# A linear-recurrence stage on one core: the first product of each level by 128x128 block matrices, and an identity added by VectorE

## What is computed

```python
def rwkv7_recurrence(r, decay, k, v, kk, a):       # 8 heads, 256 steps, 64x64 state
    def step(state, inp):
        r_t, w_t, k_t, v_t, kk_t, a_t = inp
        sa = jnp.einsum('bhij,bhj->bhi', state, -kk_t)
        state = (state * w_t[:, :, None, :]
                 + sa[..., :, None] * (kk_t * a_t)[..., None, :]
                 + v_t[..., :, None] * k_t[..., None, :])
        return state, jnp.einsum('bhij,bhj->bhi', state, r_t)
```

## Time and profile before

| what | us |
|---|---|
| median of 3 runs (2218.88 to 2220.39) | 2220.13 |
| span of the profiled execution | 2214.8 |
| around the span (median less span) | 5.3 |
| PE busy in the span | 2114.3 (95%) |
| DVE busy | 1195.3 (54%) |
| ACT busy | 766.2 (35%) |

### The profile page before, as it was taken

One profiled execution on the slowest core, in us unless ns is written; L12 is line 12 of the kernel. 1 busy time (PEld: TensorE's weight loads), 2 busy tenths in 40 slices (PEclk: granted clock), 3 DMA queues, 4 the chain that ended last, 5 costly groups with the idle time before them and its releaser, 6 DMA issues. The chain is left out here.

```text
span 2214.8 us, 34331 instructions
## 1 busy us (share of the span) xinstructions
PE 2114.3 (95%) x14251; PEld 1462.8 (66%) x14251; DVE 1195.3 (54%) x1882; ACT 766.2 (35%) x1011; POOL 16.9 (1%) x18
## 2 busy tenths in 40 slices
PE   7988999999998999999999999999999999999999
PEld 5767744333334433334437888988888888988888
DVE  5774513322222222223327876888765874888874
ACT  3553301111011100011105554556544553656543
POOL 0000000000000000000000000000000000000000
PEclk9999999999999999999999999999999999999999
DMA  9544699999999999999996555444655655444652
GB/s 373 185 165 198 258 416 430 428 431 430 431 429 430 429 430 430 428 430 431 430 427 215 191 194 167 155 147 147 199 191 186 194 190 190 152 136 133 209 191 76
DMA packets 200264, 625.87 MB, mean 283 GB/s; under 512 B 13200, under 2 KB 150352, under 8 KB 164304
## 3 DMA queue, kind: packets, MB, share of 16 engines
q1 hardware_dynamic: 197536, 622.41, 72.4%
q10 hardware_dynamic: 2608, 1.72, 0.3%
HBM read 623.05 MB, written 1.05 MB: 282 GB/s over the span
## 5 line engine op out<-in xcount | busy, mean ns | idle before, releaser
L2259 DVE TENSOR_TENSOR w_low<-ring,w_high 128x2048 fp32r<-128x2048 f32 x168 | 386.6, 2306 | 164.3 <-ACT w_high L2254 164.3
L2254 ACT ACTIVATE w_high<-ring 128x2048 fp32r<-128x2048 f32 x168 | 320.3, 1910 | 172.7 <-PE bank L2608 139.8
L2603 PE MATMUL bank<-h_both,w_high 128*128 128x512 f32 x1344 | 322.5, 392 | 0.0
L1965 PE MATMUL bank<-ring,ut 128*64 128x512 f32 x1024 | 249.3, 640 | 35.4 <-DMA ring<-in_exp_w_dram 35.4
L2603 PEld LDWEIGHTS bank<-h_both,w_high 128*128 128x128 f32 x1344 | 246.6, 188 | 48.9
L2054 ACT ACTIVATE sg<-glu 128x512 f32<-128x512 f32 x32 | 20.2, 630 | 567.6 <-DVE glu L2127 567.6
L1932 PE MATMUL bank<-ring_odd,xt 128*64 128x512 f32 x960 | 209.7, 594 | 2.9 <-DVE lin L2130 2.3
L1932 PE MATMUL bank<-ring,xt 128*64 128x512 f32 x960 | 209.3, 594 | 0.0
L1965 PEld LDWEIGHTS bank<-ring,ut 128*64 128x64 f32 x1024 | 74.2, 147 | 194.6 <-issue 132.3
L2143 DVE SCALAR_TENSOR_TENSOR xT<-bank,mod,xT 128x256 f32<-128x256 f32 x128 | 54.2, 477 | 224.4 <-PE bank L1976 224.4
L2608 PEld LDWEIGHTS bank<-h_both,w_low 128*128 128x128 f32 x1344 | 167.4, 188 | 7.0
(11 more groups left out here) (571 smaller groups left out, 2779.8 us busy)
## 6 DMA issues: line engine op xcount, KB each, us to landing
ring<-in_exp_w_dram SPq DMA_DIRECT2D x64, 2048.0 KB, 27.7
ring_odd<-in_exp_w_dram SPq DMA_DIRECT2D x64, 2048.0 KB, 27.8
ring<-in_exp_w_dram SPq DMA_DIRECT2D x128, 1024.0 KB, 25.4
ring<-in_ffn_w_gate_dram SPq DMA_DIRECT2D x44, 1024.0 KB, 5.2
ring<-in_ffn_w_up_dram SPq DMA_DIRECT2D x44, 1024.0 KB, 5.2
ring<-in_ffn_w_down_dram SPq DMA_DIRECT2D x44, 1024.0 KB, 4.9
ring<-in_w_in_dram SPq DMA_DIRECT2D x36, 1024.0 KB, 5.2
ring<-in_ada_w_dram SPq DMA_DIRECT2D x24, 1024.0 KB, 9.8
```

What stands on the lines that cost most here:

```text
L1965: ins = nc.tensor.matmul(bank[first + dh][at:at + 64, :], ut[:, r % 4, rows:rows + 64], w[:, x, 512 * dh:512 * dh + 512], start=False, sto ...
L2254: nc.scalar.activation(w_bufs[0][u % BUFS], ring2[:, u % RING2, :], ACT.Copy).then_inc(high2, 1)
L2259: nc.vector.tensor_tensor(w_bufs[1][u % BUFS], ring2[:, u % RING2, :], w_bufs[0][u % BUFS].bitcast(F32), ALU.subtract).then_inc(low2, 1)
L2603: return nc.tensor.matmul(b[:, :], w_parts[0][:, at:at + P], moving.rearrange("p a t -> p (a t)"), start=start, stop=False, skip_group_che ...
```

## The change

1. `low` becomes `low_blocks`: for each system a 128x128 matrix with the two 64x64 triangles in two quarters and zeros in the other two. It lies in the memory of `states`. GpSimd clears the zero quarters with four memsets at the stage's start; ACT writes the triangles with four copies of 64 partitions in place of two of 128.
2. `x_product` is then one product over all 128 rows in place of two over 64.
3. The groups are systems 0 to 7 and 8 to 15 (contiguous) in place of even and odd.
4. The 32 identity products are gone. DVE adds the identity while it takes the step matrices from PSUM (four instructions); ACT's eight copies are gone.
5. DVE's work on `bonus` and `gate` moves behind the first and the second `state`; ACT's clears of `states` in level 4 move behind the levels.

```diff
-                def x_product(s_, ph):
-                    return nc.tensor.matmul(place(4 + s_ % 2, inverse_rows(s_, ph), s_), low[half_rows(ph), s_, :], inv_t[half_rows(ph), s_, :],
-                                            start=True, stop=True)
+                def x_product(s_):
+                    return nc.tensor.matmul(place(4 + s_ // (NS // 2), slice(0, P), s_), low_blocks[:, s_, :], inv_t[:, s_, :], start=True, stop=True)
...
-                        pe.wait_ge(sem("low_ready"), 2)
+                        pe.wait_ge(sem("low_cleared"), 4)
+                        pe.wait_ge(sem("low_ready"), 2 * g + 2)
...
-                    for s_ in range(0, NS, 2):
+                    for s_ in range(NS // 2):
                         for ph in range(2):
                             grown = growth_t(s_, ph)
-                        for ph in range(2):
-                            ins = x_product(s_ + 1, ph)
+                        ins = x_product(NS // 2 + s_)
...
-                        for h2 in range(2):
-                            for ph in range(2):
-                                r = half_rows(ph)
-                                ins = nc.tensor.matmul(bank[6 + ph][half_rows(h2), at:at + 64], ident[r, r], ident[r, r], start=False, stop=True)
...
-                        for a in range(TT):
-                            ins = nc.scalar.activation(step_m[rows, 2 * a + ph, :, rows],
-                                                       bank[6 + ph][rows, T * a:T * a + T].rearrange("p (h j) -> p h j", h=HP), ACT.Copy)
-                        st.tell(ins, "m_taken")
...
+                dve.wait_ge(sem("cleared"), 1)
+                dve.wait_ge(sem("m_ready"), 1)
+                for ph in range(2):
+                    for h2 in range(2):
+                        rows = half_rows(h2)
+                        st.tell(nc.vector.tensor_tensor(step_m[rows, ph:NCH:2, :, rows], bank[6 + ph][rows, :].rearrange("p (a h j) -> p a h j", a=TT, h=HP),
+                                                        ident[rows, rows].unsqueeze(1).unsqueeze(1).to_broadcast([64, TT, HP, 64]), ALU.add), "m_taken")
```

More of the change, by code:

```diff
@@ L1079, in build @@
             a3, a2, a4 = lt_a3[:, :, 1, :], a2_a4[:, :, 0, :], a2_a4[:, :, 1, :]
-            low, inv, inv_t, xs = (x.rearrange("p (s t) -> p s t", t=CH) for x in ring_scratch[4:8])
+            inv, inv_t, xs = (x.rearrange("p (s t) -> p s t", t=CH) for x in ring_scratch[5:8])
             za = ring[:, SCRATCH + 2, :].rearrange("p (s x) -> p s x", s=NS)
@@ L1087, in build @@
             states = sb("states", [P, NCH, HP, P], where=c5)
+            low_blocks = states[:, :, :, :].rearrange("p c h t -> p (c h) t")
             LEVELS = 5
@@ L1105, in inverse_rows @@
             def inverse_rows(s_, ph):
-                return half_rows(ph if s_ % 2 else 1 - ph)
+                return half_rows(ph if s_ >= NS // 2 else 1 - ph)
             def group(x, g):
-                return x[:, g:NS:2, :]
+                return x[:, NS // 2 * g:NS // 2 * g + NS // 2, :]
             def chunks(ap, ph):
@@ L1114, in build, with _ @@
             SYSTEMS = [(h2, hp, a) for h2 in range(2) for hp in range(HP) for a in range(TT)]
+            @S.block.gpsimd
+            def _(gps):
+                S.clear_former(gps)
+                for g in range(2):
+                    for ph in range(2):
+                        nc.gpsimd.memset(group(low_blocks, g)[half_rows(ph), :, half_rows(ph if g == 0 else 1 - ph)], 0.0).then_inc(S.sem("low_cleared"), 1)
             @S.block.sync
@@ L1137, in place @@
                 def place(b, rows, s_):
-                    return bank[b][rows, CH * (s_ // 2):CH * (s_ // 2) + CH]
-                def x_product(s_, ph):
-                    return nc.tensor.matmul(place(4 + s_ % 2, inverse_rows(s_, ph), s_), low[half_rows(ph), s_, :], inv_t[half_rows(ph), s_, :],
-                                            start=True, stop=True)
+                    return bank[b][rows, CH * (s_ % (NS // 2)):CH * (s_ % (NS // 2)) + CH]
+                def x_product(s_):
+                    return nc.tensor.matmul(place(4 + s_ // (NS // 2), slice(0, P), s_), low_blocks[:, s_, :], inv_t[:, s_, :], start=True, stop=True)
                 def growth_t(s_, ph):
                     r = inverse_rows(s_, ph)
-                    return nc.tensor.matmul(place(2 + s_ % 2, half_rows(ph), s_), inv[r, s_, :], xs[r, s_, :], start=True, stop=True)
+                    return nc.tensor.matmul(place(2 + s_ // (NS // 2), half_rows(ph), s_), inv[r, s_, :], xs[r, s_, :], start=True, stop=True)
                 def wait_x(n, g):
@@ L1166, in growth @@
                         pe.wait_ge(sem("products_taken"), 2)
-                    for s_ in range(g, NS, 2):
+                    for s_ in range(NS // 2 * g, NS // 2 * g + NS // 2):
                         for ph in range(2):
@@ L1197, in _ @@
                 wait_x(0, 0)
-                for s_ in range(0, NS, 2):
-                    for ph in range(2):
-                        ins = x_product(s_, ph)
+                for s_ in range(NS // 2):
+                    ins = x_product(s_)
                 ins.then_inc(sem("x_ready0"), 1)
@@ L1221, in _ @@
                         wait_x(n + 1, 0)
-                    for s_ in range(0, NS, 2):
+                    for s_ in range(NS // 2):
                         for ph in range(2):
-                            grown = growth_t(s_ + 1, ph)
+                            grown = growth_t(NS // 2 + s_, ph)
                         if n + 1 < LEVELS:
-                            for ph in range(2):
-                                ins = x_product(s_, ph)
+                            ins = x_product(s_)
                     grown.then_inc(sem("growth_t1"), 1)
@@ L1261, in _ @@
                                 r = half_rows(ph)
-                                nc.tensor.matmul(bank[6 + ph][half_rows(h2), at:at + 64], za[r, system(h2, hp, a), 0:64],
-                                                 nat[r, 1, a, head_cols(h2, hp)], start=True, stop=False)
-                        for h2 in range(2):
-                            for ph in range(2):
-                                r = half_rows(ph)
-                                ins = nc.tensor.matmul(bank[6 + ph][half_rows(h2), at:at + 64], ident[r, r], ident[r, r], start=False, stop=True)
+                                ins = nc.tensor.matmul(bank[6 + ph][half_rows(h2), at:at + 64], za[r, system(h2, hp, a), 0:64],
+                                                 nat[r, 1, a, head_cols(h2, hp)], start=True, stop=True)
                 ins.then_inc(sem("m_ready"), 1)
@@ L1344, in _ @@
                 act.wait_ge(sem("low_product"), 1)
-                for h2 in range(2):
-                    st.tell(nc.scalar.activation(flat(low[:, 8 * h2:8 * h2 + 8, :]), bank[4 + h2][:, :], ACT.Copy), "low_ready")
+                for g in range(2):
+                    for ph in range(2):
+                        st.tell(nc.scalar.activation(group(low_blocks, g)[half_rows(ph), :, half_rows(1 - ph if g == 0 else ph)],
+                                                     bank[4 + g][half_rows(ph), :].rearrange("p (s t) -> p s t", t=CH), ACT.Copy), "low_ready")
                 for n in range(LEVELS):
@@ L1355, in _ @@
                     st.tell(nc.scalar.activation(a2v[:, q, :, :, :], bank[6 + q][:, :].rearrange("p (h a i) -> p h a i", h=HP, a=TT), ACT.Copy), "a2v_taken")
-                for k in range(2 * (LEVELS - 1), 12):
+                for k in range(6, 12):
                     clear(k)
@@ L1437, in _, with gate_bonus, weigh_gate @@
                     st.tell(nc.vector.tensor_copy(flat(za[:, 4 * k:4 * k + 4, :]), bank[k][:, :]), "za_taken")
[L1438 to L1443, removed]
+                def gate_bonus():
+                    for m in range(HP):
+                        ins = nc.vector.scalar_tensor_tensor(bonus[:, m, :], bonus[:, m, :], par("rwkv_gn_b", m), gate[:, m, :], ALU.add, ALU.mult)
+                    st.tell(ins, "bonus_gated")
+                def weigh_gate():
+                    dve.wait_ge(sem("bonus_gated"), 1)
+                    for m in range(HP):
+                        nc.vector.tensor_scalar(gate[:, m, :], gate[:, m, :], par("rwkv_gn_g", m), None, ALU.mult)
                 dve.wait_ge(sem("out_squares"), 1)
@@ L1453, in _ @@
                                                     chunk_decay[:, :, c:c + 1].to_broadcast([P, HP, 64]), ALU.mult), "state_ready")
+                    if c == 0:
+                        gate_bonus()
+                    elif c == 1:
+                        weigh_gate()
                 dve.wait_ge(sem("out_root"), 1)
```

5 lines of the change are left out of this document (1 added, 4 removed).

## The result

The changed kernel takes 2272.51 us (median, 2268.68 to 2280.15), the kernel before 2219.51 us in the same series: a ratio of 1.0244, 95% interval 1.0225 to 1.0262. The forecast was 2249 with a range of 2238 to 2258. The direction was right, the size was not: 53 us slower where 29 were worked out. The profiled execution has a span of 2271.0 us, 56.2 more than before's 2214.8.

What follows compares the result with a forecast made beforehand. PE waiting for its own instructions, 256 in some 3.6 us, was taken to bound the levels. Terms 29.4 + 0.5 - 0.9 = +29.0 us gave a span of 2243.8, median 5.3 above: 2249.1 us, range 2238 to 2258.

Steps and rivals of the forecast that it cites:

- Bound by refills of instructions: Levels before the change: PE waits for its own instructions, 256 of them in some 3.6 us; this bound falls away after.
- A system 0.62 us, a change of shape 0.14 us: Block of x_product and growth_t: 0.117 + 0.224 + two shape changes of 0.14; a block of eight 4.97 instead of 0.93 us.
- Rival 1: Levels: refills stay the bound and fewer instructions pay, -6.3 us, 2213.8 us, or 2217 with part of the gain; 6%.
- rival 2: Blocks of the levels: shapes change without a drain when no wait stands between; +9.4 in all, 2229.5 us; 7%.
- The levels +29.4 us: First block to values(1): 27.0 us before, 56.4 after, from slower blocks plus 0.5 for mask and copy waits.
- Rival 3: PE's clock falls in the levels as products are sparser: 2300 us at worst, +1.7 for one piece; 4% for over 2258.
- First product +0.5: Product standing alone ahead of the levels: 16 full records take 1.8 us where 16 quarter products took 1.2; +0.5 us.
- Identity by VectorE: Behind the levels: 32 identity products gone from PE, eight times 0.117 us, -0.93 us.
- 0 for the refills: Two instruction pauses behind the levels: first may become two of some 1.6 us, second is covered; 0, ends -2.9 to +3.2.
- DVE, ACT, GpSimd and the moved work at nothing: DVE's additions, ACT's copies, GpSimd's memsets, bonus and gate lie off the path: 0; additions 2.7 us if uncovered.

Runs made afterwards that it cites:

- one-column run: Kernel before with one more product of one moving column, same weights, ahead of each growth product (128 products); 2228.5 us, ratio 1.0044.

## Why the prediction failed where it did

- **Bound by refills of instructions**: it fits the traces, and the pauses did end as forecast (no "issue" idle in the levels after). The one-column run can't confirm that instructions rather than products set the 3.6 us; the sum does not need it, as it put nothing down for fewer instructions in the levels.
- **A system 0.62 us, a change of shape 0.14 us**: right. 0.63 at full clock; 0.141 and 0.146 for a change from three kernels. Rival 1 needed a half level of 2.25 us and rival 2 a block of 2.73; at full clock the changed kernel took 5.83 and 4.96.
- **The levels +29.4 us**: the term that failed; the direction was right, the size was half of what was measured. It was worked out throughout at the granted clock of 1.00, from rows at 1.00. At that clock the sum holds (56.0 us for 56.4); with 71.7 us at 0.50 the levels took 57.8 us more in place of 29.4.
- **Rival 3, the clock, at 4%**: the step behind it was wrong. It read the earlier trace rows as a clock that falls after an idle time, noted that "No idle of that length would arise", and left the sparser products as a half sentence. The clock did fall, the second time with no idle since 156.08, and stayed down for 64.86 us. Its end of 2300 us was a fair bound, but 4% and a range up to 2258 were not. What could have raised the chance: before's levels had 64 records in 1.14 us, and the change spends 45% of each system's time (0.28 of 0.62) on changes of shape. The rows read from before had no such stretch at any clock, so its 1.00 said nothing of this order.
- **First product +0.5**: right. ACT's first copy of X starts 5.86 us after the stage's first ACT work (149.37 to 155.23), before 5.38 by the same measure.
- **Identity by VectorE**: -0.93 for the products as forecast (L1263's 64 records alone, 1.16 us). "0 for the refills" was mis-sized: the second pause went, as said, but the first became one longer pause and not two of 1.6. -2.1 in all by the traces of two kernels, -3.9 (1.8 to 5.8) by the medians of one.
- **DVE, ACT, GpSimd and the moved work at nothing**: right. DVE's additions end at 250.90, PE's first reader starts at 255.67; `bonus` lies before DVE's wait of 3.23 us.

The Trainium skill, TensorE: Matmul & The Clock Gate, Part 1, ties the half clock to how busy PE has been. The rows here go half way with it: the clock did change with the work that PE was given, but PE's records filled 64.86 of 64.86 us while the clock was 0.50, so "busy" as the profile counts it did not tell whether the clock would stay.

## What to carry to other kernels

Fewer and larger products were no gain by themselves in this fp32 kernel: one full product of 64 columns cost 0.224 us where the two quarter products that it replaced cost 0.058 beside others, and each change between the two forms cost 0.14 us more. If forms must mix, try putting all of one form together: the same work in two changes for a block instead of 16 took 2226 us in place of 2272, still more than the 2218 of before. When a change makes PE's work sparser, do the sum at half clock too: half-level times differed by 1.67 between the two levels, and a PE row that is busy all the time is no sign that the clock will hold.

## What the runs showed of the hardware

- The granted clock fell to 0.50 and stayed there for 64.86 us while PE's records left no gap. It stayed at 1.00 with two changes of shape in a block of 3.0 us, was down for 10 us with eight, for 13.5 with sixteen and full products twice, for 71.7 with sixteen and single ones; and for most of the levels with two changes and 16 products of one column (0.58 on average from 182 to 277 us). The kernels with eight changes and with the full products twice fell only once, in the first block, and ran the same order at 1.00 afterwards; why they stayed up is open.
- In the changed kernel it came back once, at 165.4 us, behind `growth` and `products`, in which 64x64 products follow each other without a change; at 175.6 us, before the second block from there was through, it was down again.
- Half clock cost a factor of 1.67 on a half level, not 2, although PE's records had no gap.
- A full-form fp32 product of one column took nearly as long as one of 64: a system with it 0.59 us, with 64 columns 0.63.
- In two quarters of the array, too, a product of one column took as long as one of 64: two and two of them 0.23 us, two of 64 alone 0.117.
